# Expert layers of a two-block transformer kernel: 128-row waves multiplied in high and low weight parts, down products two groups behind

## The reference

```python
logits = t @ w_router                       # 256 x 8
top_v, top_i = lax.top_k(logits, 2)
gates = softmax(top_v)
for e in range(8):                          # wg, wu: 1024 x 3584, wd: 3584 x 1024, fp32
    w_e = sum(where(top_i == e, gates, 0))
    out = out + w_e[:, None] * ((silu(t @ wg[e]) * (t @ wu[e])) @ wd[e])
```

## Time and profile before

| | us |
|---|---|
| median of 3 executions | 2171.69 |
| profiled execution, its own time | 2174.48 |
| its span in the trace | 2172.7 |
| PE busy | 1919.0 (88%) |
| DVE busy | 602.3 (28%) |
| ACT busy | 525.2 (24%) |
| POOL busy | 443.3 (20%) |
| read from HBM over the span | 479.49 MB, of it 352 MB expert weights |
| first expert weight load issued / first expert product | 1182.1 / 1233.6 |

### The profile page before, as it was taken

The page is one execution under the profiler, slowest core; times in us unless marked ns, Lnnn a source line. Parts: engine busy times, 40 slices in busy tenths (PEclk is TensorE's granted clock), DMA queues, the critical chain, the costliest instruction groups (busy, mean ns, idle before and its releaser), DMA issues.

```text
span 2172.7 us, 23440 instructions
## 1 busy us (share of the span) xinstructions
PE 1919.0 (88%) x9741; PEld 1137.9 (52%) x9742; DVE 602.3 (28%) x1156; ACT 525.2 (24%) x859; POOL 443.3 (20%) x257
## 2 busy tenths in 40 slices
PE   4999678969799997987978799999988999988887
PEld 2787426957577775877855443343333333333332
DVE  3942545652300003443035420111111100211113
ACT  3322225542312121233235120101111110211021
POOL 0421463531333342425453000000000000000000
PEclk8998879979899998998999899999999999999999
DMA  8344000022254452234422689879999976999995
GB/s 327 127 158 158 1 0 1 24 94 78 67 199 161 156 200 109 97 111 97 123 68 84 245 351 410 333 271 347 419 405 419 397 306 264 385 416 409 415 409 238
DMA packets 147112, 482.29 MB, mean 222 GB/s; under 512 B 23284, under 2 KB 48229, under 8 KB 132661
## 3 DMA queue, kind: packets, MB, share of 16 engines
q1 hardware_dynamic: 146000, 477.82, 57.8%
q10 hardware_dynamic: 997, 2.75, 0.3%
HBM read 479.49 MB, written 1.05 MB: 221 GB/s over the span
## 4 chain that ended last, share of the span: by engine, by line
PE 57%; DMA 10%; DVE 5%; SPq 3%; ACT 2%; issue 1%; POOL 1%; DVEq 0%; ACTq 0%
PE PS L2347 19%; DMA BIG<-in_od_exp_wu 9%; PE PS L1852 8%; PE PS L1853 8%; PE PS L1854 8%; PE PS L2397 6%; SPq L575 2%; PE PS L2266 1%; DMA BIG<-in_od_exp_wd 1%; PE PS L2321 1%; PE PS L2338 1%; PE PS L1831 1%; DVE HB L1255 1%; PE PS L2312 1%; PE PS L2176 1%
## 5 line engine op out<-in xcount | busy, mean ns | idle before, releaser
L2347 PE MATMUL PS<-BIG,QB 128*64 128x448 f32 x2560 | 505.3, 553 | 38.0 <-DMA BIG<-in_od_exp_wu 22.1
L2347 PEld LDWEIGHTS PS<-BIG,QB 128*64 128x64 f32 x2560 | 182.9, 139 | 340.7 <-issue 334.7
L2397 PE MATMUL PS<-BIG,QB 128*64 128x512 f32 x1120 | 252.9, 610 | 18.4 <-issue 16.0
L616 POOL TENSOR_TENSOR BIG_parts<-BIG,QB_parts 128x2048 fp32r<-128x2048 f32 x33 | 152.7, 4628 | 282.7 <-ACT QB_parts L793 282.7
L2397 PEld LDWEIGHTS PS<-BIG,QB 128*64 128x64 f32 x1120 | 80.7, 140 | 184.6 <-issue 183.5
L616 POOL TENSOR_TENSOR BIG_parts<-BIG,BIG_parts 128x2048 fp32r<-128x2048 f32 (+1 forms) x28 | 126.1, 4502 | 248.4 <-ACT BIG_parts L793 248.4
L1853 PE MATMUL PS<-HB_parts,QB_parts 128*128 128x512 f32 x352 | 137.3, 390 | 0.0
L1853 PE MATMUL PS<-BIG_parts,BIG_parts 128*128 128x512 f32 (+1 forms) x336 | 127.3, 379 | 0.0
L1769 DVE TENSOR_TENSOR HB<-HB,PS 128x512 f32<-128x512 f32 x32 | 21.8, 688 | 310.0 <-PE PS L2321 308.9
L1852 PE MATMUL PS<-ZS_parts,BIG_parts 128*128 128x512 f32 (+1 forms) x240 | 92.4, 385 | 10.0 <-DVEq L1265 8.1
L1854 PE MATMUL PS<-BIG_parts 128*128 128x512 f32 (+1 forms) x256 | 95.8, 374 | 0.0
(11 more groups left out here) (357 smaller groups left out, 2933.0 us busy)
## 6 DMA issues: line engine op xcount, KB each, us to landing
BIG<-in_od_exp_wg SPq DMA_DIRECT2D x64, 1792.0 KB, 19.3
BIG<-in_od_exp_wu SPq DMA_DIRECT2D x64, 1792.0 KB, 21.1
BIG<-in_od_exp_wd SPq DMA_DIRECT2D x64, 1792.0 KB, 21.5
BIG<-in_ada_w SPq DMA_DIRECT2D x24, 2048.0 KB, 8.2
BIG<-in_od_w_qkv SPq DMA_DIRECT2D x6, 2048.0 KB, 8.6
BIG<-in_ev_ffn_wg SPq DMA_DIRECT2D x11, 1024.0 KB, 8.9
BIG<-in_ev_ffn_wu SPq DMA_DIRECT2D x11, 1024.0 KB, 11.4
BIG<-in_ev_ffn_wd SPq DMA_DIRECT2D x5, 2048.0 KB, 8.5
```

Of the source, the lines that this page charges most:

```text
L616: pool.tensor_tensor(r12(w), w, r12(high), ALU.subtract).then_inc(split_l, 1)
L2347: last = mm(PS[at:at + 64, bank, 0:GROUP], XG[:, 4 * part + k, r0:r0 + 64], wgu[u][:, k, GROUP * c:GROUP * c + GROUP], start=(part + k == ...
L2397: last = mm(PS[64 * n:64 * n + 64, bank, :], HET[:, 7 * q + k, r0:r0 + 64], halves_of[i][:, a, :], start=(q + k == 0), stop=(q == NPAIR - ...
```

## The change

- Chunk order and down products: the chunks now come as gate/up of pairs 0 and 1, down 0, gate/up 2, down 1, gate/up 3, down 2, down 3, and PE does the down products of pair p-1 right after the gate/up products of pair p.
- In 128-row waves, gate and up products are made as three fp32r products of a 128-column stationary block each (`gate_up_split`): (high x, high w), (high x, low w), (low x, high w). 64-row waves keep the fp32 products on half arrays (`gate_up_pairs`).
- The parts of the weights are made slice by slice (one k, one group, gate and up: 128x896) in every wave, of 64 rows too: ACT writes the high part (`high`), DVE subtracts it from the chunk in fp32r and writes the low part (`low`). Three buffers `HIGHS` hold the parts, so slice n may be made once PE and DVE have finished slice n-3. A chunk's slot is free once PE and DVE are both through with it.
- The gathered tokens get parts as well (`gathered_high`, `gathered_low`), each with its first 64 columns repeated so that gate and up land on opposite halves.
- `ACC` is gone: DVE multiplies each scattered result with `GE` in PSUM and adds it to `X` (`scattered`), eight operations instead of four. The scatter in wave 0 is left out. The clearing of `ACC` and the final addition of `ACC` go.
- The final norm's gain `FG` is loaded after the last wave, by ACT's queue. `expert_slot` starts one slot later, so 4 and not 5 chunks are loaded before the first wait for `out1`.
- ACT and DVE have seven waves written out, like PE. `SEL`, `SELT`, `RTB`, `HE`, `GE` move to other buffers.

```diff
+        def high(w, p, part, c, ks=range(4), first=False):
+            if 0 in ks:
+                for u in range(2):
+                    act.wait_ge(*chunk_at(w, p, part, u)[0])
+            for k in ks:
+                if not first:
+                    act.wait_ge(e_grp, replaces(w, p, part, c, k))
+                    act.wait_ge(e_low, replaces(w, p, part, c, k))
+                v, to, _ = weights(p, part, c, k)
+                act.activation(r12(to), v, ACT.Copy).then_inc(e_high, 1)
...
+        def low(w, p, part, c, ks=range(4)):
+            for k in ks:
+                v, from_, to = weights(p, part, c, k)
+                dve.wait_ge(e_high, piece(w, p, part, c) + k + 1)
+                dve.tensor_tensor(r12(to), v, r12(from_), ALU.subtract).then_inc(e_low, 1)
...
+        def scattered(n, last=False):
+            for i in range(4):
+                cols = slice(512 * (i % 2), 512 * (i % 2) + 512)
+                dve.wait_ge(e_sc, 4 * n + i + 1)
+                seq(dve.tensor_tensor(PS[:, SCB[i], :], PS[:, SCB[i], :], GE[:, cols], ALU.mult))
+                ins = dve.tensor_tensor(X[:, i // 2, cols], X[:, i // 2, cols], PS[:, SCB[i], :], ALU.add)
...
         PE, per wave
+                def gate_up_split(p, part, c):
+                    for k in range(4):
+                        start, stop = part + k == 0, part == 1 and k == 3
+                        _, w_high, w_low = weights(p, part, c, k)
+                        pe.wait_ge(e_low, piece(w, p, part, c) + k + 1)
+                        for u in range(2):
+                            high, low = (r12(v[:, 4 * part + k, 64 * u:64 * u + P]) for v in (XGH, XGL))
+                            to, w_h, w_l = PS[:, 2 * u + c, 0:GROUP], r12(w_high[:, u, :]), r12(w_low[:, u, :])
+                            mm(to, high, w_h, start=start, stop=False)
+                            mm(to, high, w_l, start=False, stop=False)
+                            last = mm(to, low, w_h, start=False, stop=stop)
+                        last.then_inc(e_grp, 1)
...
+                        for c in range(2):
+                            with pe.If(more > 0):
+                                gate_up_split(p, part, c)
+                            with pe.If(more < 1):
+                                gate_up_pairs(p, part, c)
...
+                    if p:
+                        down(p - 1)
+                gather(w + 1, 0)
+                columns(NPAIR - 1)
+                gather(w + 1, 1)
+                down(NPAIR - 1)
...
         DVE, per wave (ACT's has the same shape, with silu, hidden_columns and take_out)
+                low(w, 0, 0, 0, range(3, 4))
+                low(w, 0, 0, 1)
+                if scatter:
+                    scattered(w)
+                low(w, 0, 1, 0)
+                low(w, 0, 1, 1)
+                for p in range(NPAIR - 1):
+                    multiply(2 * p)
+                    low(w, p + 1, 0, 0, range(3))
+                    multiply(2 * p + 1)
+                    low(w, p + 1, 0, 0, range(3, 4))
+                    low(w, p + 1, 0, 1)
+                    ...
```

More of the change, by code:

```diff
@@ L1715, in _ @@
             seq(last)
+            low(0, 0, 0, 0, range(3))
             select(slice(0, 1), 1)
@@ L1782, in _ @@
                         dve.wait_ge(e_tr, w + 1)
                         for kind in range(2):
[L1784 to L1797 removed]
+                            select(col, kind)
@@ new lines, in wave @@
+                    low(w, p + 1, 1, 0)
+                    low(w, p + 1, 1, 1)
+                multiply(NGR - 2)
+                multiply(NGR - 1)
+                take_rows(w + 1)
+                if ahead:
+                    gathered_low(w + 1)
+                    low(w + 1, 0, 0, 0, range(3))
+            for w in range(E - 1):
+                wave(w, slice(w + 1, w + 2), w > 0, w < E - 2, True)
+            dve.wait_ge(rt_tab, 2)
+            waves = dve.value_load(RI[0:1, 0:1], min_val=E, max_val=WAVES)
@@ L1800, in _ @@
+            with dve.Fori(E - 1, waves) as w:
+                wave(w, bass.ds(w + 1, 1), True, False, False)
+            dve.wait_ge(e_add, 4 * waves)
+            scattered(waves, last=True)
             dve.wait_ge(fin_x, 2)
@@ L2328, in _, with wave @@
             pe.wait_ge(rt_ev, KINDS_EV)
-            def wave(w, more):
+            pe.nop().then_inc(e_sc, 4)
+            def wave(w, more, scattering):
                 def columns(p):
@@ new lines, in gate_up_pairs, with down, rows @@
+                def gate_up_pairs(p, part, c):
+                    for k in range(4):
+                        w_full, _, _ = weights(p, part, c, k)
+                        for u in range(2):
+                            last = mm(PS[64 * u:64 * u + 64, 2 * u + c, 0:GROUP], XG[:, 4 * part + k, 0:64],
+                                      w_full[:, u, :], start=(part + k == 0), stop=(part == 1 and k == 3))
+                        last.then_inc(e_grp, 1)
+                def down(q):
+                    halves_of = []
+                    for i in range(2):
+                        where, view = chunk_at(w, q, "down", i)
+                        pe.wait_ge(*where)
+                        halves_of.append(view.rearrange("p (a n) -> p a n", n=512))
+                    pe.wait_ge(e_htev, NPAIR * w + q + 1)
+                    def rows(bank, r0):
+                        for i in range(2):
+                            for a in range(7):
+                                k, n = (7 * i + a) // 2, (7 * i + a) % 2
+                                last = mm(PS[64 * n:64 * n + 64, bank, :], HET[:, q % 2, k, r0:r0 + 64],
+                                          halves_of[i][:, a, :], start=(q + k == 0), stop=(q == NPAIR - 1 and k == 6))
+                        return last
+                    with pe.If(more > 0):
+                        rows(7, 64)
+                    rows(6, 0).then_inc(dn_mm, 1)
@@ L2364, in wave @@
-                        last = gate_up(0, 0, part, wgu)
-                        if part:
-                            last.then_inc(e_grp, 1)
-                        if p and part == 0:
-                            pe.wait_ge(e_h, NGR * w + 2 * p)
-                        if p + part == 0:
-                            pe.wait_ge(e_gev, 2 * w + 2)
-                        gate_up(1, 0, part, wgu).then_inc(e_grp if part else gu_mm, 1)
+                        for u in range(2):
+                            pe.wait_ge(*chunk_at(w, p, part, u)[0])
```

255 lines of the change are left out of this document (143 added, 112 removed).

## The result

The kernel after takes 2180.25 us (median of 5 executions, 2179.95 to 2182.79) against 2171.69 (5 executions, 2169.62 to 2174.55): ratio 1.0042, interval 1.0031 to 1.0053. It is slower by 8.6 us; 2176.0 had been forecast. The profiled execution took 2182.23 us with a span of 2180.4, against 2174.48 and 2172.7.

What follows compares the result with a forecast made beforehand. Loads were taken to bound most waves, PE the 128-row ones. Wave 0 +11.5, 128-row waves with followers -8.8 and tail +2.4 made +5, taken as +4: 2174.5 profiled becomes 2178.5, so 2176 us predicted, range 2162 to 2193.

Steps and rivals of the forecast that it cites:

- Price of a slice: In 128-row waves, six fp32r products of 448 columns at 0.200 us each: 1.20 us a slice (1.12 to 1.36).
- Rival A: Products without overhead, 1.12 us a slice, loop keeps up and clock does not fall: 2163 to 2167; chance 0.22.
- B: Rival: three-buffer loop binds or weight loads are exposed after waits, 1.27 to 1.33 us a slice: 2185 to 2193; chance 0.24.
- The loop: Three weight-part buffers pass PE, ACT, DVE, PE with three hand-overs: 3.5 us for three slices, 1.17 each.
- 128-row waves: Waves 1 and 4: products, scatter place, waits and copies sum to -11.1 us each, 158.5 becoming 147.4.
- The scatter place: In 128-row waves, DVE's eight operations and a low part before PE goes on: 4.85 becomes 7.6 us, +2.8.
- the spell at half clock: After PE's 3.5 us stand at the scatter of a 128-row wave, PE at 1.2 GHz: up to +1.7 us.
- Pair 0 to 1: In 128-row waves, no down products cover silu and DVE's two operations between pairs 0 and 1: +1.6 us.
- The wave after it: Follower of a 128-row wave: slots come free only after DVE's subtractions, so loads stand idle 6.7 us.
- Wave 0: First 64-row wave: DVE's and ACT's part-making delays freed slots and loads, +11.5 us; ends some 10 us later.
- Other 64-row waves: DVE busy some 91 of 107.9 us, but seven loaded chunks cover 31 us of delay: no cost.
- Tail: After the last landing, pair 2's downs (7.9), gathers and transposes stand before pair 3: 10.2 against 7.85 us, +2.4.

Runs made afterwards that it cites:

- the square: Kernel after and the kernel without parts, each with eight scatter operations (2180.25, 2185.65 us) or with YE scaled once before the scatter (2168.81, 2173.91 us).

## Why the prediction came out as it did

Its direction and most of its mechanism held; the median was 4.25 us above the forecast, inside the range, and the profiled execution 3.7. By its own steps:

- **Price of a slice.** 1.21 to 1.24, not 1.20; with 1.29 to 1.35 at each group's start the mean of undisturbed slices is 1.25, so the forecast had 64 x 0.05 = 3.2 us per 128-row wave too little. The interpolation (0.200 a product) was good, 0.2025 measured; what it had no term for is the 0.1 us at a group's start. Rival A (1.12) and B (1.27 and more) are both out. The loop as such was shown with two buffers.
- **128-row waves.** The forecast's wave holds its first slice's wait of 2.1, which by my cuts falls into the wave ahead (waves 0 and 3); without it the forecast was 158.5 - 13.2 = 145.3, measured 150.0 and 148.3. The scatter place was right: 7.62 us from 1353.20 to 1360.82, 7.6 forecast. **Two terms are mis-sized: the price of a slice, by 3.2 us in each of the two waves, and the spell at half clock**, 1.7 forecast; measured (excess of its slices over 1.25 each) 1.6 + 2.7 = 4.3 us in wave 1, where there are two spells, and 2.4 in wave 4. Pair 0 to 1 cost 0.92 + 0.50 = 1.4 (1.6), the copy of the hidden columns 3 x 0.3 = 0.9 (1.5). For wave 1 that is 3.2 + 2.6 - 0.2 - 0.6 = 5.0, where 4.7 us are to be explained, for wave 4 it is 3.1 of 3.0.
- **The wave after it.** +7.4 and +6.8, forecast +6.7, with slots freed within 0.6 us of the forecast's list. (The 96 to 99 us that were to be its sign are less than 93.1 + 6.7; the waves took 100.5 and 100.3.) The run with parts in waves 1 and 4 alone shows the cause for 5.4 and 3.2 of it; the runs of the square give the scatter's share in DVE's chain, some 3.
- **Wave 0.** +12.1; the forecast was "some 10 us later", and 11.5 for the loads. The run without parts in wave 0 shows that the parts made in it cost 12.0, with the wait for the first slice of wave 1 in both lengths. That wait (2.57 us, 0.90 before) is about made up by the rest of the change, which without parts makes wave 0 shorter by 1.6 us (96.9). The forecast's slots come free 2 us later than the real ones.
- **Other 64-row waves.** "No cost" was nearly right: wave 6 has +0.4. Of the +2.0 in wave 3 the parts made at most 0.8, and the longer wait for the first slice of wave 4 (2.90 us, 1.02 before) is not its cause either: with parts in waves 1 and 4 alone and a wait of 0.71 the wave took 109.8 us, with no parts at all 109.1. The cause stayed open. DVE is busy for 84 to 87 us there (91 forecast).
- **Tail.** +0.1, not +2.4: the pair of down products after the wait ran at full clock (1.6 less) and what stands between the pairs took 4.6 and not 5.1. The term was wrong because I gave a spell to an idle of 2 us, where the earlier trace rows show one behind an idle of 2.41 and none behind one of 1.99.
- **The sum.** In my cuts the forecast's +4.0 reads, wave by wave: 12.5, -13.2, 6.7, 2.1, -13.2, 6.7, 0, tail 2.4. Measured: 12.1, -8.5, 7.4, 2.0, -10.2, 6.8, 0.4, 0.1, and -2.4 for the earlier start of wave 0, in all 7.7. So the forecast of the 128-row waves was 7.7 us too low and that of the tail 2.3 too high, and 2.4 us were taken off by a start that no step of the change explains; that the total was only 4 off is partly luck.

What the prediction did not see at all is that the change consists of two things of opposite sign: it costed the scatter's eight operations (2.8 + 1.7 in the wave, 2.75 us in the follower's chain) inside sums with the parts and never by itself. Its own terms add up to 14.5 us for the two pairs of waves. Alone the operations were measured at 11.4 to 11.7 us (12 by the ratios), at least twice what the parts save.

## What to carry to other kernels

A buffer is free when its slowest reader is through: giving a second engine work on each loaded chunk moves every load behind that engine's queue, so make derived operands only for the waves that use them. Scale a small tensor once before it is spread, not each spread result; four short operations on the engine that PE and the ring both wait for were worth 11.5 us. When a change moves several things, price each alone and not only the waves they end up in: here one was a gain and one a loss, and taken apart, with parts only where they are used, they gave 21 us.

## What the runs showed of the hardware

- TensorE's granted clock did not follow the stalls alone. It fell to its 1.2 GHz level for 3 to 6 us after stalls of 2.57 and of 2.94 and 0.58 us, did not fall after one of 2.90 in the same execution, and fell in the run with small products in the gaps after stalls of 0.53 and 0.26. With the scatter's stalls cut to 0.78 and 0.66 us it stayed up, in all six such waves of three runs. In this kernel a stall of some 3 us on PE has to be priced at its length plus 0 to 2.8 us.
- The three fp32r products in place of one fp32 product save under a fifth: 1.25 us a slice of 128 rows against 24.27/16 = 1.52 in the earlier trace rows.
- 36 branches a wave on PE, in place of 4, left nothing that the times can tell (2180.25 and 2179.44 us, ratios 1.0042 and 1.0031 with intervals that overlap).
